# A six-mixer stack on one core: squares ahead of weight conversions at the begin, two row tiles normalised by ScalarE and GpSimd at the end

## The reference

```
rms_norm(x, w)      = x * rsqrt(mean(x*x) + 1e-6) * w                    # first step of the kernel
layer_norm(x, g, b) = (x - mean(x)) * rsqrt(var(x) + 1e-5) * g + b       # last step of the kernel
```

## Time and profile before

| | |
|---|---|
| time, median of 3 runs | 2522.47 us (2522.42 to 2524.73) |
| profiled execution, its own time | 2522.69 us |
| its span, first to last instruction | 2521.0 us |
| TensorE busy | 2379.8 us, 94% of the span |
| VectorE, ScalarE, GpSimd busy | 993.4, 890.3, 935.3 us |
| mean granted TensorE clock | 0.977 of full speed |

### The profile page before, as it was taken

One profiled execution on the slowest core, in us unless ns is written; L12 is line 12 of the kernel. 1 busy time (PEld: TensorE's weight loads), 2 busy tenths in 40 slices (PEclk: granted clock), 3 DMA queues, 4 the chain that ended last, 5 costly groups with the idle time before them and its releaser, 6 DMA issues.

```text
span 2521.0 us, 33172 instructions
## 1 busy us (share of the span) xinstructions
PE 2379.8 (94%) x13336; PEld 1923.6 (76%) x13336; DVE 993.4 (39%) x1771; ACT 890.3 (35%) x1372; POOL 935.3 (37%) x706
## 2 busy tenths in 40 slices
PE   5999999999999979999999989999999999999996
PEld 4877787868768967877786657888888888888885
DVE  4634245235635533643314774511102354412204
ACT  3334334243433553334423443422222323322311
POOL 3333344133410013341343231644554554554542
PEclk9999999999989979999999999999999999999998
DMA  4332222023210013323222121233232333233231
GB/s 123 87 67 67 77 84 84 34 42 106 84 50 2 3 34 68 76 76 59 78 84 84 34 67 51 84 100 100 82 119 86 99 100 101 85 99 100 83 127 58
DMA packets 136738, 191.82 MB, mean 76 GB/s; under 512 B 30992, under 2 KB 84624, under 8 KB 136608
## 3 DMA queue, kind: packets, MB, share of 16 engines
q1 hardware_dynamic: 127296, 183.61, 24.8%
q10 hardware_dynamic: 9312, 6.35, 0.9%
HBM read 187.84 MB, written 2.10 MB: 75 GB/s over the span
## 4 chain that ended last, share of the span: by engine, by line
issue 63%; POOL 31%; PE 4%; DVE 1%; DMA 0%; POOLq 0%; ACT 0%; SPq 0%; ACTq 0%
POOL weights_low L644 31%; PE bank L668 1%; PE bank L670 1%; PE bank L669 1%; DMA weights_raw<-in_fox_w_in_dram 0%; POOLq L649 0%; DVE row_statistics L2248 0%; DVE x L2272 0%; DVE x L2274 0%; DVE x L2298 0%; POOLq L642 0%; ACT weights_high L1536 0%; SPq L531 0%; ACT L1536 0%; DVE row_statistics L2267 0%
## 5 line engine op out<-in xcount | busy, mean ns | idle before, releaser
L644 POOL TENSOR_TENSOR weights_low<-weights_raw,weights_high 128x512 fp32r<-128x512 f32 x688 | 932.6, 1387 | 1551.2 <-ACT weights_high L1536 1551.2
L668 PE MATMUL bank<-xt_high,weights_high 128*128 128x512 f32 (+1 forms) x1600 | 611.5, 382 | 16.8 <-POOL weights_low L644 12.7
L670 PE MATMUL bank<-xt_high,weights_low 128*128 128x512 f32 (+1 forms) x1600 | 599.4, 375 | 0.0
L669 PE MATMUL bank<-xt_low,weights_high 128*128 128x512 f32 (+1 forms) x1600 | 599.0, 374 | 0.0
L1536 ACT ACTIVATE weights_high<-weights_raw 128x2048 fp32r<-128x2048 f32 x172 | 329.0, 1914 | 685.7 <-PE bank L670 675.6
L668 PEld LDWEIGHTS bank<-xt_high,weights_high 128*128 128x128 f32 x1600 | 304.1, 190 | 86.3 <-POOL weights_low L644 24.9
L670 PEld LDWEIGHTS bank<-xt_high,weights_low 128*128 128x128 f32 x1600 | 303.3, 190 | 54.4
L669 PEld LDWEIGHTS bank<-xt_low,weights_high 128*128 128x128 f32 x1600 | 304.0, 190 | 50.0
L668 PE MATMUL bank<-weights_high,xt_high 128*128 128x512 f32 x512 | 206.4, 403 | 6.0 <-DVE xt_low L2285 2.8
L670 PE MATMUL bank<-weights_high,xt_low 128*128 128x512 f32 x512 | 200.8, 392 | 0.0
L669 PE MATMUL bank<-weights_low,xt_high 128*128 128x512 f32 x512 | 200.2, 391 | 0.0
(11 more groups left out here) (390 smaller groups left out, 2993.6 us busy)
## 6 DMA issues: line engine op xcount, KB each, us to landing
weights_raw<-in_fox_w_in_dram SPq DMA_DIRECT2D x64, 512.0 KB, 5.8
weights_raw<-in_ffn_w_gate_dram SPq DMA_DIRECT2D x44, 512.0 KB, 4.0
weights_raw<-in_ffn_w_up_dram SPq DMA_DIRECT2D x44, 512.0 KB, 4.9
weights_raw<-in_ffn_w_down_dram SPq DMA_DIRECT2D x40, 512.0 KB, 4.4
weights_raw<-in_gla_w_in_dram SPq DMA_DIRECT2D x24, 512.0 KB, 4.1
weights_raw<-in_gdn_w_in_dram SPq DMA_DIRECT2D x24, 512.0 KB, 4.5
weights_raw<-in_attn_w_qkv_dram SPq DMA_DIRECT2D x24, 512.0 KB, 4.3
weights_raw<-in_conv_w_in_dram SPq DMA_DIRECT2D x24, 512.0 KB, 4.6
```

What stands on the lines that cost most here:

```text
L644: pool.tensor_tensor(w_lo[:, odd, k], raw[:, odd, k], w_hi[:, odd, k].bitcast(F32), ALU.subtract)\
L668: pe.matmul(out_ap, lh, rh, start=first, stop=False)
L669: pe.matmul(out_ap, lh, rl, start=False, stop=False)
L670: return pe.matmul(out_ap, ll, rh, start=False, stop=last)
```

## The change

At the begin: SP issues tiles 0 and 1 of `x`, slot 0, tiles 2 and 3, slot 1, in this order. On ScalarE's queue the norm weights come first, ahead of the four small vectors, and all five ahead of any other ScalarE work. ScalarE then squares tiles 0 and 1 with their roots, rounds slot 0, copies the transposes of tiles 0 and 1, squares tiles 2 and 3 with their roots, rounds slot 1, and copies tiles 2 and 3. TensorE's, VectorE's and GpSimd's streams are as before at the begin.

At the end: for tiles 0 and 1 VectorE makes only the factors; ScalarE applies (x - mean)/sigma to the whole tile (one activation of 128x1024), and GpSimd, whose stream had ended with the last `split`, multiplies by the gain and adds the bias (two tensor_tensor of 128x1024 per tile). Tiles 2 and 3 stay with VectorE, each now finished before the next is begun. SP waits for tiles 0 and 1 by a new semaphore.

The middle of the kernel has the same instructions in the same order: in VectorE's code the branch for the other stages is only moved.

```diff
         @block.sync
-            for tt in range(TT):
-                sp.dma_start(x[:, tt], t["x"][0, tt * P:tt * P + P]).then_inc(x_loaded[tt], 16)
+            def load_rows(*tiles):
+                for tt in tiles:
+                    sp.dma_start(x[:, tt], t["x"][0, tt * P:tt * P + P]).then_inc(x_loaded[tt], 16)
+            load_rows(0, 1)
             def load_slot(pair, odd, parts):
                 if not (isinstance(pair, int) and pair == 0):
                     sp.wait_ge(w_split, 8 * pair - 4 + 4 * odd)
+                elif odd:
+                    load_rows(2, 3)
...
                     for tt in range(TT):
-                        sp.wait_ge(out_rows, tt + 1)
+                        if tt < 2:
+                            sp.wait_ge(early_rows, tt + 1)
+                        else:
+                            sp.wait_ge(out_rows, tt - 1)
...
         @block.gpsimd
+            pool.wait_ge(rows_loaded, 16 * n_norm_loads)
+            for tt in range(2):
+                pool.wait_ge(rows_ready, TT * (stages[-1]["filled"] // 8) + tt + 1)
+                pool.tensor_tensor(x[:, tt], x[:, tt], norm_w[:], ALU.mult).then_inc(pool_step, 1)
+                pool.wait_ge(pool_step, 7 + tt)
+                pool.tensor_tensor(x[:, tt], x[:, tt], norm_b[:], ALU.add).then_inc(early_rows, 1)
...
         @block.scalar
-            for odd in range(2):
-                weights_high(0, odd)
+            load_norm("rms", 0, False)
...
-                    if not joined:
-                        load_vectors_and_norm()
...
+                    if st["last"]:
+                        all_slots_high()
+                        for tt in range(2):
+                            root_of_variance(tt)
+                            act.wait_ge(row_factors, st["ln"] + tt + 1)
+                            act.activation(x[:, tt], x[:, tt], ACT.Identity, bias=soft[:, 8 + tt:9 + tt],
+                                           scale=stat[:, 8 + tt:9 + tt]).then_inc(rows_ready, 1)
+                        root_of(2)
+                        root_of(3)
+                        continue
+                    if not joined:
+                        squares_of(0)
+                        root_of(0)
+                        squares_of(1)
+                        root_of(1)
+                        weights_high(0, 0)
+                        transposed_high(0)
+                        transposed_high(1)
+                        for tt in (2, 3):
+                            squares_of(tt)
+                            root_of(tt)
+                        weights_high(0, 1)
+                        for tt in (2, 3):
+                            transposed_high(tt)
+                        continue
...
         @block.vector
-                    if norm in ("ln1", "ln2"):
-                        for tt in range(2):
-                            add(tt)
-                            statistics(tt)
-                        for tt in range(2):
-                            normalise_rows(tt)
...
+                    if st["last"]:
+                        add(0)
+                        variance(0)
+                        add(1)
+                        factors(0)
+                        variance(1)
+                        factors(1)
                         for tt in (2, 3):
                             add(tt)
                             statistics(tt)
+                            normalise_rows(tt)
+                        continue
```

More of the change, by code:

```diff
@@ L250, in six_mixer_stack @@
     n_pairs = total["pair"]
+    n_norm_loads = sum(0 if st["norm"] == "plain" else 1 if st["norm"] == "rms" else 2 if st["last"] else 4
+                       for st in stages if st["kind"] in ("fill", "join"))
     ctx = ExitStack()
@@ L396, in six_mixer_stack @@
         row_factors = sem("row_factors_ready")
+        early_rows = sem("early_output_tile_normalised")
         residual_rows = sem("residual_tile_scaled")
@@ L426, in six_mixer_stack @@
             "lam_in", "lam_out", "copied", "rotated", "v_taken", "scores", "max", "exps", "mixed", "turned", "turned_used", "weighed",
-            "out_taken", "squares", "sums", "means", "roots", "normed", "rows", "rows_turned")}
+            "out_taken", "squares", "sums", "means", "roots", "normed", "rows_turned")}
         fox_rsqrt = sem("fox_head_norms_done")
@@ L1706, in _ @@
                     root_of(1)
-                    if joined:
-                        weights_high(st["pair"] + n_slots // 2, 0)
+                    weights_high(st["pair"] + n_slots // 2, 0)
                     transposed_high(0)
                     transposed_high(1)
-                    if joined:
-                        weights_high(st["pair"] + n_slots // 2, 1)
+                    weights_high(st["pair"] + n_slots // 2, 1)
                     for tt in (2, 3):
@@ L2355, in _ @@
                         continue
-                    if norm in ("ln1", "ln2"):
-                        for tt in range(2):
-                            add(tt)
-                            statistics(tt)
-                        for tt in range(2):
-                            normalise_rows(tt)
-                        for tt in range(2):
-                            transposed_low(tt)
+                    if st["last"]:
[5 more added lines that the diff above has]
+                        factors(1)
                         for tt in (2, 3):
@@ L2366, in _ @@
                             statistics(tt)
[L2367 to L2371, removed]
-                            normalise_rows(tt)
-                        transposed_low(0)
-                        add(2)
-                        add(3)
-                        transposed_low(1)
-                        for tt in (2, 3):
-                            statistics(tt)
+                            normalise_rows(tt)
+                        continue
+                    add(0)
+                    add(1)
+                    for tt in range(2):
+                        statistics(tt)
+                        normalise_rows(tt)
+                    transposed_low(0)
+                    add(2)
+                    add(3)
+                    transposed_low(1)
+                    for tt in (2, 3):
+                        statistics(tt)
                     for tt in (2, 3):
```

## The result

The changed kernel takes 2505.6 us (median of 4 runs, 2505.01 to 2506.48), the kernel before beside it 2522.44 (4 runs, 2517.88 to 2524.73): ratio 0.9947, 95% interval 0.9934 to 0.9959. That is 16.8 us. The forecast was 2509.6, a gain of 12.9. The profiled execution of the changed kernel took 2505.89 us, with a span of 2504.2; span against span the gain is also 16.8 us.

What follows compares the result with a forecast made beforehand. The prediction took a late square, root, normalise, transpose chain on ScalarE's queue to bound the begin and VectorE alone the end: 2522.7 - 12.1 - 0.8 = 2509.8, less 0.2 for the median, 2509.6 us; range 2505 to 2514.

Steps and rivals of the forecast that it cites:

- the bounds 4.5 and 7.1: Begin: first tile of x lands at 4.5 us if not held up, 7.1 behind ScalarE's other loads; 5.8 taken.
- the 7.7 of the working: Begin: 7.7 us from the first square to VectorE's pass over tile 1, 10.0 before; tile 1 ready at 13.5.
- 12.0 us, within 10.0 and 12.6: Begin: when slot 0's load lands, with two x tiles fewer but norm weights and small vectors ahead of it.
- this rounding is thus hidden: Begin: ScalarE rounds slot 0 from 12.0 to 13.9 us, while it would wait for tile 1's transposes until 15.6.
- the 5.96 of the working: Begin: 5.96 us from tile 1's pass to the end of the last root of tiles 2 and 3, at 19.4.
- Slot 1 as the new bound: Begin: slot 1 is rounded by 21.4 us and split by 27.4, with TensorE waiting; the half pair ends at 30.9.
- Rival (c): Begin: dearer wait for slot 1, by TensorE's slow pitch or late roots; begin gains 8 us, 2513.7 total; 14 in 100.
- the 12.1: Begin: forecast gain of 12.1 us, the first half pair ending at 30.9 instead of 43.03.
- The turns: End: GpSimd and VectorE alternate whole instructions, delaying tile 2's passes 3.7 us; 0.8 us gain taken instead of 4.2.
- Rival (b): End: GpSimd's wide instructions don't block VectorE or finish before 2503.6; gain 4.2 us, 2506.2 total; 15 in 100.
- Rival (e): Middle: gives back the begin's gain if granted clock returns later after the shift; near 2520 us; 4 in 100.
- One of its signs of being wrong: Middle: the distance from the first half pair's end (43 us, then 31) to the last add should stay unchanged.

Runs made afterwards that it cites:

- e9: The changed kernel once more, with no edit: 2507.6 us (median of 5), ratio 0.9962 to the kernel before.
- e1: The kernel before with only the changed begin, its end as before: 2512.52 us (median of 12), ratio 0.9961.
- e3: The changed kernel with VectorE's wide passes of tile 2 placed behind tile 3's add and statistics: 2508.73 us (median of 6), ratio 0.9945.
- e4: The changed kernel with GpSimd's four 128x1024 instructions at the end cut into eight of 128x512: 2506.66 us (one execution).
- e5: The changed kernel with the four small vectors issued only behind the rounding of slot 1: 2505.35 us (median of 10), ratio 0.9949.
- e7: The changed kernel with small vectors behind slot 1's rounding and VectorE's tile 2 wide passes behind tile 3's statistics: 2502.14 us (median of 6), ratio 0.9931.
- x-first runs: Two runs of the changed kernel with all four tiles of x issued ahead of slot 0: 2510.32 us each, ratios 0.9973 and 0.9974.
- e8: The kernel before, profiled once more with no edit: 2525.9 us (one execution).

## Why the prediction was right, point by point

**The whole.** 12.9 us were forecast, the change itself is worth 10 to 11.5: 9.8 + 1.5 = 11.3 by the two first profiles; (42.2 - 33.6) + 1.5 = 10.1 by the means of the three profiles with the old begin and the five with the changed one (changed, e9, e1, e3, e4); 10.2 to 11.5 by times within the upper group of the clock. The first medians lie 16.8 us apart, as the profiled executions do, and there 5.4 us are the granted clock of the middle, which differed between two profiles of the kernel before too. The forecast's 2509.6 is 4 us above the first median for that reason and not for a lack in the change; by the second measurement (2507.6) it is 2 us above. The change by itself fell 1.6 us short of the forecast, 11.3 for 12.9. That the first median came out below the forecast, near the lower end of the range, is luck: the clock of the middle gave more than the change lacked.

**x and tile 1.** x landed at 7.0 in the first profile (6.3 to 6.7 in e5, e7, e9 and the x-first runs), near the upper of the bounds 4.5 and 7.1 and above the 5.8 taken. (The upper bound is 4.5 + 2.5 = 7.0 by its own working.) From the first square to the end of the pass over tile 1 it took 7.67 us, the 7.7 of the working. The first table load lay ahead of the wait for x, as taken. The second ended at 9.49 and the root ran at 9.51, which the row had told for the kernel before. The Trainium skill (ScalarE: Activation LUTs, What ACT_TABLE_LOAD costs) has another 1.38 us of drain at such a switch; this trace doesn't show them, with 0.02 us between the load's end and the root.

**Slot 0: the term that was mis-sized.** "12.0 us, within 10.0 and 12.6" was 14.5, outside its bounds, and "this rounding is thus hidden" fell with it. The small vectors were counted by the share of the DMA engines that they took the earlier trace rows, and by that 2.5 us at most, together with the norm weights. e5 shows that they alone cost slot 0 at least 2.9 us; without them slot 0 is there before 11.62, and the rounding is hidden as described. The chain from there is the forecast's with 2.3 us more: last root's end 21.7 (19.4), slot 1 rounded 23.5 (21.4), split 29.6 (27.4), half pair 33.2 (30.9). TensorE's first weight matmul, forecast near 16, started at 18.34. Of the 2.3 us, 1.2 would have come from x alone, since tile 1 was ready at 14.72 instead of 13.5; the other 1.0 is slot 0's: from tile 1's pass to the end of the last root it took 7.0 us instead of the 5.96 of the working, which e5 has. In e9 x was there 0.7 us earlier and the half pair ended no sooner (33.29): where slot 0 is late, it alone sets the begin. With the small vectors out of the way (e5) the half pair ends at 31.4, and the 0.5 us left are those by which x landed later than taken (6.3 for 5.8).

**Slot 1 as the new bound.** Right in each link: TensorE waits for weights_low up to 29.6; GpSimd's four splits take 5.98 beside one wide pass of VectorE, 0.98 more than the 5.00 of slot 0 (1 us taken); 3.55 us from the last quarter for 3.4. The slow pitch lasted for twelve matmuls behind the first where nine were taken, which slot 1's wait hid. Rival (c) had put the begin at 8 us by a dearer wait for slot 1; what is missing from the 12.1 came from slot 0 instead. Its fall of TensorE's pitch after the waits is seen in e7 alone, for 1.2 us.

**The end.** 1.5 us for 0.8. The turns are as worked out. GpSimd's instruction takes 2.34 to 2.40 us where 2.5 was taken, the third ends earlier against VectorE's pass, and 2.8 us are lost where 3.7 had been counted. The estimate of 2.3, half of the 4.5 us that the Trainium skill (GPSIMD Engine Reference, Elementwise — side-by-side cycle accounting) gives for 2048 values, was the closer one. The Trainium skill (SBUF — State Buffer, SBUF: two separate sides) calls the port pair an exclusive lock, held for a whole instruction; the trace agrees, since each of VectorE's two passes ends 1.08 us after the GpSimd instruction that it waited for, and so does the first one in e3 (2502.17 after 2501.09). Rival (b), no blocking, fell by the trace of the changed kernel itself, and e3 and e4 moved the loss with order and size as turns would have it. Without the turns the end would have gained 1.5 + 2.8 = 4.3 us, rival (b)'s 4.2; e3 has 4.7, with the roots' waits hidden too.

**The middle.** Rival (e) had the right quantity and the wrong cause: the granted clock did change the middle, by 5 us and in this case for the better, and by chance. That the middle differs by several us between two profiles of one kernel stood nowhere in the forecast. One of its signs of being wrong did appear: the distance from the end of the first half pair to the first add of the last layer norm was to stay, and it went from 2446.8 to 2441.4 us. By e8 that sign tells nothing of the change, as the distance isn't fixed for one kernel either: there it is 2451.1.

## What to carry to other kernels

Ask of each small load at the begin how many packets it is, not only how many bytes: moved ahead of a large load that the chain waits for, it cost here 2.9 us of that load's landing for 0.7 us of the engines' time. When an engine that shares a port gets work, place the other's wide passes behind it, or cut its instructions: here the order of two loops was worth 3.2 us, and the work moved to other engines 1.5. And before crediting a change of a few microseconds, compare milestones in the untouched part of the two traces, and times at one granted clock.

## What the runs showed of the hardware

- The mean granted clock of an execution of this program lies between 0.975 and 0.982, and the time moves with it by some 6 us between 0.979 or more and 0.977 or less. The differences arise in three stretches: from the 3rd to the 31st rounding (419.5 to 421.6 us), from the 31st to the 49th (412.7 to 418.3) and from the 80th to the 87th (185.3 to 192.0).
- Two slow pitches look alike in the timeline. At TensorE's start, behind the long idle begin, matmuls of 512 columns come every 0.43 us (512 columns in 0.43 us are 1.2 GHz), for 6 to 13 matmuls in the twelve traces and 6 or 9 in two of one kernel, while the profile's granted clock shows 1.00 (18 to 22 us of the changed kernel). In e7 the same pitch, after waits of 1.24 and 0.28 us, goes with a granted clock of 0.62.
- With 1344 packets of 0.04 MB in all on one queue, the two loads of 512 KB on another on which slot 0 depends came 2.9 us or more later (14.56 and 14.66 with them, 11.62 and 11.70 or sooner without).
- A GpSimd tensor_tensor of 128x1024 in fp32 took 2.34 to 2.40 us undisturbed, two of 128x512 2.55. A VectorE pass with two operands in SBUF, 1.28 us alone, took up to 3.24 us beside them.
